# Expert slots of a two-layer diffusion backbone: the down products inside gate and up, two banks and two buffers for the rows, another order of the splits, and adaLN loads behind the reload of X

## The reference

```python
def _moe(h, router_w, router_bias, w_gate, w_up, w_down):
    ...
    for e in range(N_EXPERTS):
        he = jax.nn.silu(h @ w_gate[e]) * (h @ w_up[e])
        y = y + comb[:, e:e + 1] * (he @ w_down[e])
    return y
...
    x = x + g1 * yx                                   # the mixer
    hx = _rmsnorm(x, norm_ffn[i]) * (1 + sc2) + sh2   # adaLN, per layer
    x = x + g2 * y                                    # the experts
```

## Time and profile before

| | |
|---|---|
| three runs | 1175.56, 1180.86, 1182.62 us |
| profiled execution | 1180.38 us, of which 1178.6 are its span |
| TensorE busy | 1097.4 us (93%), granted clock 0.973 on average |
| VectorE busy | 821.6 us (70%) |
| ScalarE busy | 497.7 us (42%) |
| GpSimd busy | 201.3 us (17%) |
| expert slots, layer 0 | from about 222 to 483 us |
| expert slots, layer 1 | from about 925 us to the end |

### The profile page before, as it was taken

How to read it: one execution, slowest core, us unless ns; L and a number is a source line. 1 busy time by engine, 2 the same in 40 slices (tenths; PEclk the granted TensorE clock), 3 DMA queues, 4 the chain that set the end, 5 groups by cost and what they waited for, 6 DMA issues and landing times.

```text
span 1178.6 us, 16659 instructions
## 1 busy us (share of the span) xinstructions
PE 1097.4 (93%) x4819; PEld 806.0 (68%) x4820; DVE 821.6 (70%) x985; ACT 497.7 (42%) x681; POOL 201.3 (17%) x139
## 2 busy tenths in 40 slices
PE   4999899899999999579999999999999999999993
PEld 2554347577777777257888888878887677767772
DVE  5896985788888988355344344453565888888884
ACT  5210214376767676431111111141223466656662
POOL 2111111123333234100000000000000123223341
PEclk9999899899999999879999999999999999999997
DMA  9869549566979981603632233313235877988742
GB/s 361 330 242 384 212 178 415 198 232 184 338 235 345 343 224 24 237 16 127 251 124 93 82 111 125 125 54 124 85 131 202 343 222 267 372 295 282 209 92 34
DMA packets 82538, 243.03 MB, mean 206 GB/s; under 512 B 10592, under 2 KB 35384, under 8 KB 73276
## 3 DMA queue, kind: packets, MB, share of 16 engines
q1 hardware_dynamic: 62436, 188.88, 42.1%
q0 software_dynamic: 18496, 48.31, 16.3%
q10 hardware_dynamic: 1560, 5.26, 1.2%
HBM read 220.39 MB, written 40.89 MB: 222 GB/s over the span
## 4 chain that ended last, share of the span: by engine, by line
PE 65%; DVE 11%; DMA 10%; issue 8%; ACT 2%; ACTq 2%; DVEq 1%; POOL 0%; POOLq 0%
PE PS L1954 15%; PE PS L1835 7%; PE PS L2061 7%; PE PS L2065 7%; PE PS L2062 7%; DMA out_dram<-YO,TOKI 6%; PE PS L1967 3%; DVE ACC L1134 3%; PE PS L1973 3%; PE PS L1944 3%; PE PS L1686 2%; PE PS L1648 2%; PE PS L1848 2%; DMA WAE<-in_w_ada_dram 1%; PE PS L1863 1%
## 5 line engine op out<-in xcount | busy, mean ns | idle before, releaser
L1455 DVE TENSOR_TENSOR WL<-RAW,WH 128x1024 fp32r<-128x1024 f32 x204 | 240.1, 1220 | 26.0 <-ACT WH L922 24.9
L922 ACT ACTIVATE WH<-RAW 128x1024 fp32r x196 | 196.6, 1052 | 50.2 <-issue 36.7
L1954 PE MATMUL PS<-WH,XTH 128*128 128x512 f32 x384 | 154.0, 401 | 8.9 <-DVE XTL L1448 4.7
L2061 PE MATMUL PS<-HTH,WINH 128*128 128x512 f32 x384 | 150.8, 393 | 5.7 <-DVE HTL L1568 5.4
L1954 PE MATMUL PS<-WH,XTL 128*128 128x512 f32 x384 | 150.3, 391 | 0.0
L2062 PE MATMUL PS<-HTL,WINH 128*128 128x512 f32 x384 | 149.9, 390 | 0.0
L1954 PE MATMUL PS<-WL,XTH 128*128 128x512 f32 x384 | 149.8, 390 | 0.0
L2065 PE MATMUL PS<-HTH,WINL 128*128 128x512 f32 x384 | 118.7, 390 | 0.0
L1954 PEld LDWEIGHTS PS<-WH,XTH 128*128 128x128 f32 x384 | 72.1, 188 | 27.3 <-issue 13.4
L648 POOL DMA_INDIRECT XG<-h_dram,TOKI x54 | 68.1, 1261 | 113.8 <-DVE TOKI L1405 55.1
L2061 PEld LDWEIGHTS PS<-HTH,WINH 128*128 128x128 f32 x384 | 72.3, 188 | 22.3 <-DVE HTL L1568 4.8
(11 more groups left out here) (247 smaller groups left out, 1811.4 us busy)
## 6 DMA issues: line engine op xcount, KB each, us to landing
RAW<-in_moe_w_gate_dram SPq DMA_DIRECT2D x32, 1024.0 KB
RAW<-in_moe_w_up_dram SPq DMA_DIRECT2D x32, 1024.0 KB
WDR<-in_moe_w_down_dram SPq DMA_DIRECT2D x32, 1024.0 KB
WA<-in_w_ada_dram SPq DMA_DIRECT2D x28, 1024.0 KB, 8.3
WAE<-in_w_ada_dram SPq DMA_DIRECT2D x12, 1024.0 KB, 9.7
WINR<-in_conv_w_in_dram SPq DMA_DIRECT2D x24, 512.0 KB, 3.8
SLAB<-in_w_ada_dram SPq DMA_DIRECT2D x8, 1024.0 KB, 10.5
X<-x_dram SPq DMA_DIRECT2D x16, 512.0 KB, 5.9
```

The costliest lines, as they stand in the source:

```text
L922: nc.scalar.activation(piece_of(WH[par], i), raw_piece(at, i), ACT.Copy).then_inc(w_high, 1)
L1455: V.tensor_tensor(piece_of(WL[par], i), raw_piece(e, i), piece_of(WH[par], i).bitcast(f32), ALU.subtract).then_inc(w_low, 1)
L1954: ins = T.matmul(bank(2), x[:, ch, :], w[par][:, :, ch, :], start=ch == 0 and i == 0, stop=ch == NC - 1 and i == 2)
L2061: T.matmul(bank(b), WINH[par][:, ch, :], HTH[:, ch, cols], start=ch == 0, stop=False)
```

## The change

TensorE: the row transposes run one slot further ahead (s+2), gate and up of odd and even slots write different banks (2 and 6), and their four pieces are spread: piece 0, hidden transposes of s-1, piece 1, down products of s-1, pieces 2 and 3, row transposes of s+2. XTH and XTL get a second buffer. ScalarE and VectorE take the splits in another order, all four weight pieces of s+1 in slot s, WDH and WDL of s instead of s-1. Behind layer 0's slots SP issues the two adaLN loads after the reload of X, VectorE waits for the bias only before the first adaLN sum, GpSimd's clearing of ACC waits for WDL's semaphore as well, and TensorE's mixer columns wait for all HE (bank 6 is theirs).

The diff, cut to its core (the prologues and the unrolled last slots follow the same order, and skipped slots raise the semaphores to match):

```diff
+    XTL = [XTL0, r.put("XTL1", [P, NC, P], f32r)]
+    XTH = [r.put("XTH0", [P, NC, P], f32r), XTH1]
+    def gated_bank(par):
+        return bank(6 if par else 2)
 # SP
                 sp.wait_ge(w_low, PIECES * MAX_SLOTS)
-                load_ada_pair(2, 0)
                 sp.wait_ge(moe_done, 1)
                 sp.wait_ge(cols_mm, 2)
                 for m in range(NT):
                     sp.dma_start(X[:, m, :], x_dram[0][m * P:(m + 1) * P, :]).then_inc(x_back[m], 16)
+                load_ada_pair(2, 0)
 # GpSimd
                 pool.wait_ge(yd_mm, MAX_SLOTS)
+                pool.wait_ge(wd_low, MAX_SLOTS)
                 bias_row(1, 2 * D)
 # ScalarE
+            def het_high_of(s):
                 act.wait_ge(he_tr, s + (b + 1))
                 nc.scalar.activation(HETF[:], bank(3)[:, P:2 * P], ACT.Copy).then_inc(het_full, 1)
                 nc.scalar.activation(HETH[:], bank(3)[:, 0:P], ACT.Copy).then_inc(het_high, 1)
             def slot(s, par):
-                down_high(s - 1)
-                weights_high(s + 1, 1 - par, (2, 3))
-                gate(s)
-                xt_high(s + 1)
-                weights_high(s + 2, par, (0, 1))
+                weights_high(s + 1, 1 - par, (0,))
+                het_high_of(s - 1)
+                weights_high(s + 1, 1 - par, (1, 2, 3))
+                down_high(s)
+                gate(s, par)
+                xt_high(s + 2, par)
 # VectorE
             def body(s, par, free=True):
-                e0, e1, e2 = expert_of(s - 1), expert_of(s + 1), expert_of(s + 2)
+                e0, e1 = expert_of(s), expert_of(s + 1)
+                weights_low(s + 1, 1 - par, e1, (0,))
                 het_split(s - 1)
-                down_low(s - 1, e0)
-                weights_low(s + 1, 1 - par, e1, (2, 3))
+                weights_low(s + 1, 1 - par, e1, (1, 2))
+                y_evac(s - 1, 1 - par, free)
+                weights_low(s + 1, 1 - par, e1, (3,))
+                down_low(s, e0)
                 gated(s, par)
-                xt_low(s + 1)
-                weights_low(s + 2, par, e2, (0, 1))
-                y_evac(s - 1, 1 - par, free)
+                xt_low(s + 2, par)
-                dve.wait_ge(bias_in, 32)
 ...
                 taps(0, 0)
+                dve.wait_ge(bias_in, 32)
                 ada_pair(0, 2, 0, False)
 # TensorE
+            def transposes(s, par, nth, first=False):
                 pe.wait_ge(gathered[layer][par], nth * 16)
+                if not first:
+                    pe.wait_ge(xt_dve, s + b0)
+            def gate_up(s, par, pieces=range(PIECES), first=False):
+                if 0 in pieces:
+                    if not first:
+                        pe.wait_ge(he_ready, s + (b0 - 1))
+                    pe.wait_ge(xt_act, s + (b0 + 1))
+                    pe.wait_ge(xt_dve, s + (b0 + 1))
+                for piece in pieces:
+                    pe.wait_ge(w_low, s * PIECES + (b0 * PIECES + piece + 1))
 ...
             def slot(s, par, next_nth, more=True, last=False):
                 e = expert_of(s - 1)
+                if not last:
+                    gate_up(s, par, (0,))
                 pe.wait_ge(he_ready, s + b0)
                 hidden_transposes(s - 1, 1 - par)
                 if not last:
-                    gate_up(s, par)
-                if more:
-                    transposes(s + 1, 1 - par, next_nth)
+                    gate_up(s, par, (1,))
                 pe.wait_ge(yo_ready, s + (b0 - 1))
                 down(s - 1, e)
+                if not last:
+                    gate_up(s, par, (2, 3))
+                if more:
+                    transposes(s + 2, par, next_nth)
 ...
-            gate_up(0, 0)
             transposes(1, 1, 1)
+            gate_up(0, 0, first=True)
+            transposes(2, 0, 2)
 ...
+                pe.wait_ge(he_ready, MAX_SLOTS)
                 mixer_columns()
```

More of the change, by code:

```diff
@@ L235, in backbone @@
     WL = [r.put(f"WL{i}", [P, 2, NC, FF], f32r) for i in range(2)]
-    XTL = r.put("XTL", [P, NC, P], f32r)
+    XTL0 = r.put("XTL0", [P, NC, P], f32r)
     SG = r.put("SG", [P, FF])
@@ L909, in _, with xt_high @@
             b = layer * MAX_SLOTS
-            def xt_high(s):
+            def xt_high(s, par):
                 act.wait_ge(xt_tr, s + (b + 1))
-                nc.scalar.activation(XTH[:].rearrange("p c n -> p (c n)"), bank(0, 2),
+                nc.scalar.activation(XTH[par][:].rearrange("p c n -> p (c n)"), bank(0, 2),
                                      ACT.Copy).then_inc(xt_act, 1)
@@ L952, in _ @@
                 act.wait_ge(he_ready, b)
-            nc.scalar.activation(SG[:], bank(2)[:, 0:FF], ACT.Silu).then_inc(silu_g, 1)
-            xt_high(1)
-            weights_high(2, 0, (0, 1))
+            nc.scalar.activation(SG[:], gated_bank(0)[:, 0:FF], ACT.Silu).then_inc(silu_g, 1)
+            xt_high(2, 0)
+            down_high(0, first=True)
             with act.Fori(0, ALWAYS) as i:
@@ L1443, in gated, with xt_low @@
                 dve.wait_ge(silu_g, s + (b + 1))
-                V.tensor_tensor(HE[par][:], SG[:], bank(2)[:, FF:2 * FF], ALU.mult).then_inc(he_ready, 1)
-            def xt_low(s):
+                V.tensor_tensor(HE[par][:], SG[:], gated_bank(par)[:, FF:2 * FF], ALU.mult).then_inc(he_ready, 1)
+            def xt_low(s, par):
                 dve.wait_ge(xt_act, s + (b + 1))
-                V.tensor_tensor(XTL[:].rearrange("p c n -> p (c n)"), bank(0, 2),
-                                XTH[:].rearrange("p c n -> p (c n)").bitcast(f32),
+                V.tensor_tensor(XTL[par][:].rearrange("p c n -> p (c n)"), bank(0, 2),
+                                XTH[par][:].rearrange("p c n -> p (c n)").bitcast(f32),
                                 ALU.subtract).then_inc(xt_dve, 1)
@@ L1945, in transposes @@
                 ins.then_inc(xt_tr, 1)
-            def gate_up(s, par):
-                pe.wait_ge(xt_act, s + (b0 + 1))
-                pe.wait_ge(xt_dve, s + (b0 + 1))
-                for ch in range(NC):
-                    if ch % 2 == 0:
-                        pe.wait_ge(w_low, s * PIECES + (b0 * PIECES + ch // 2 + 1))
-                    for i, (x, w) in enumerate(((XTH, WH), (XTH, WL), (XTL, WH))):
-                        ins = T.matmul(bank(2), x[:, ch, :], w[par][:, :, ch, :],
-                                       start=ch == 0 and i == 0, stop=ch == NC - 1 and i == 2)
-                ins.then_inc(gu_mm, 1)
+            def gate_up(s, par, pieces=range(PIECES), first=False):
+                if 0 in pieces:
+                    if not first:
+                        pe.wait_ge(he_ready, s + (b0 - 1))
[3 more added lines that the diff above has]
+                    pe.wait_ge(w_low, s * PIECES + (b0 * PIECES + piece + 1))
+                    for ch in (2 * piece, 2 * piece + 1):
+                        for i, (x, w) in enumerate(((XTH, WH), (XTH, WL), (XTL, WH))):
+                            ins = T.matmul(gated_bank(par), x[par][:, ch, :], w[par][:, :, ch, :],
+                                           start=ch == 0 and i == 0, stop=ch == NC - 1 and i == 2)
+                if PIECES - 1 in pieces:
+                    ins.then_inc(gu_mm, 1)
             def hidden_transposes(s, par):
@@ L1993, in _ @@
                 pe.wait_ge(mixer_ready, 1)
[L1994 removed]
+            transposes(0, 0, 1, first=True)
             keep_running(2, 4)
[L1996 removed]
             transposes(1, 1, 1)
+            gate_up(0, 0, first=True)
+            transposes(2, 0, 2)
             keep_running(2, 4)
             e = expert_of(0)
+            gate_up(1, 1, (0,), first=True)
             pe.wait_ge(he_ready, 1 + b0)
             hidden_transposes(0, 0)
[L2003 to L2004 removed]
+            gate_up(1, 1, (1,), first=True)
             down(0, e)
[L2006 removed]
+            gate_up(1, 1, (2, 3), first=True)
+            transposes(3, 1, 2)
+            slot(2, 0, 3)
             with pe.Fori(1, ALWAYS) as i:
                 slot(2 * i + 1, 1, i + 2)
[L2009 removed]
+                slot(2 * i + 2, 0, i + 3)
             used = slots_used(pe)
@@ L2020, in _ @@
             with pe.If(used > 2 * n):
-                slot(MAX_SLOTS - 2, 1, n + 2)
+                slot(MAX_SLOTS - 2, 1, 0, more=False)
                 slot(MAX_SLOTS - 1, 0, 0, more=False)
```

94 lines of the change are left out of this document (46 added, 48 removed).

## The result

The changed kernel takes **1191.74 us** (median of four runs, 1190.13 to 1194.56), the kernel before 1180.27 with the run taken beside it (1175.56 to 1182.62): a ratio of 1.0109, 95% interval 1.0082 to 1.0135. Forecast were 1196.7, range 1160 to 1211. The profiled execution took 1190.13 us, of which 1188.3 are its span, so it is compared with the span of 1178.6 before: 9.7 more.

What follows compares the result with a forecast made beforehand. TensorE, 93% busy, was taken to bound the kernel before; after the change, a ring through ScalarE at 10.55 us a slot. 1180.4 + 13.9 (layer 0) + 5.9 (layer 1) - 3.5 (behind layer 0) = 1196.7 us, range 1160 to 1211.

Steps and rivals of the forecast that it cites:

- Part 1: TensorE's own order in a slot: 9.77 us if nothing else waits, with 3.93 from row transposes to down products.
- Part 2: ScalarE's new order, the deciding term: down products 4.31 us after the row transposes; round 10.15, with extras 10.55.
- the ring: Row transposes, XTH, first WH, HETF, down products, 12 more products, next row transposes: one round per slot, 10.15 us.
- The loop's start: ScalarE's loop starting over every second slot, between XTH and WH: 0.6 us taken, 0.3 per slot.
- rare long waits: ScalarE's occasional long waits ahead of WH, no longer covered: about 0.1 us per slot.
- Part 3: VectorE's slot: HE done 12.6 us after the row transposes, just when wanted; level with the ring, no cost by itself.
- Part 4: Rows, gathers, stores: XTL wait goes, no cost; slot 3's row transposes at 245.7 and 948.5.
- Part 5: Ends of the expert stages: last YO 8.7 us after the last row transposes; layer 0 +13.9, layer 1 +5.9.
- Part 6: Behind layer 0's slots: loads 1.3, bias wait 1.0, clock 1.2, together -3.5 us; TensorE's new wait covered by 1.5.
- TensorE as the bound (1160): Rival: HETF is not held up by WH and the loop start, slots of 9.77 us, 1160 us; chance 0.22.
- the ring at its floor (1180): Rival: the loop's start is hidden by the wait for row transposes, round about 10.15 us, 1180 us; chance 0.23.
- VectorE falling behind (1211): Rival: VectorE's register loads and long waits add to ScalarE's, round 10.9 us, 1211 us; chance 0.1.

Runs made afterwards that it cites:

- e3: Changed kernel with ScalarE's HETF and HETH copies ahead of the first WH and VectorE's HETL ahead of its WL: 1170.88 us, ratio 0.993.
- e7: e1 with VectorE's last WL (piece 3) moved ahead of YO: 1173.02 us, ratio 0.9948.
- e2: Changed kernel with two WH copies instead of one ahead of HETF on ScalarE: 1238.29 us, ratio 1.0495.
- e4: Changed kernel with ScalarE's loop over the first eight pairs of slots written out: 1187.41 us, ratio 1.0079.
- e1: Changed kernel with gate-and-up piece 2 moved ahead of the down products on TensorE: 1191.96 us, ratio 1.0109.
- e10: Changed kernel with layer 1's down weights of experts 3 to 15 loaded for 16 columns of 1024, for measuring alone: 1193.69 us, ratio 1.0131.
- e11: Kernel before with layer 1's down weights of experts 3 to 15 loaded for 16 columns of 1024, for measuring alone: 1170.91 us, ratio 0.9935.
- e5: Kernel before with only the two adaLN loads moved behind the reload of X and the bias wait moved to the first adaLN sum: 1175.35 us, ratio 0.9966.
- e6: Changed kernel with the adaLN loads and the bias wait left as in the kernel before: 1196.97 us, ratio 1.0143.
- e8: e3 with GpSimd's gather of slot s+5 ahead of the store of slot s: 1171.24 us, ratio 0.9931.
- e12: e3 with VectorE's last WL (piece 3) ahead of YO: 1167.72 us, ratio 0.9921.
- e9: e3 with layer 1's down weights of experts 3 to 15 loaded for 16 columns of 1024, for measuring alone: 1165.64 us, ratio 0.9899.

## Why the prediction was right

The mechanism named as deciding was the one that decided. The range by itself says little, as it was wide enough for every rival; what confirms the forecast is the signs it gave: TensorE idle for HETF in front of the down products (0.23 and 0.63 us in turn, where I had written 0.4 and 1.0), slots of 10.5 us, and no wait for XTL. The sum by its steps:

- **Part 1**, TensorE's own 9.77 us: 9.78 in e3 and e7, in the plain loops, where nothing else binds.
- **Part 2**, the ring. T to XTH 1.09 forecast, 1.07 measured; to WH 1.70, measured 1.72; to HETF 1.00, measured 0.96; to the down products 0.52, measured 0.53: 4.31 against 4.28. The down products then took 3.20 and not 3.10 (their first row 1.98 where it was 1.88), the last 12 products 2.75: 10.23, forecast 10.15. The loop's start was the term mis-sized: 0.40 where I took 0.6, between the bounds of 0.22 and 0.9. The two errors offset each other: 10.42 in the plain loops, forecast 10.45. e2 (longer ring, slower), e3 (ring opened, 9.78) and e4 (loop's start removed) show it from three sides.
- The last 0.1 of the round, rare long waits, held by luck. The stages' means of 10.50 and 10.49 are 0.08 above 10.42, but from another cause: no idle time of ScalarE ahead of the first WH in the plain loops was over 1.16 us. The 0.08 is mostly the loops with an If, whose start cost 0.7 to 0.9 and not 0.40 (idle 1.36 to 1.63 there against 0.69).
- The sentence on the Trainium skill, "Runtime: NRT & Kernel Launch", section "Instruction fetch mechanics": a stall of 1.2 us at every loop start (a size from my longest wait, the page gives none), which would have made 1205, was not there. The extra is 0.40 in the plain loops and up to 0.9 in those with an If; whether fetching instructions is in it, no run shows.
- **Part 3**, VectorE "level with the ring": too pessimistic by 0.9. HE starts at T + 11.23 in the changed kernel (302.81 to 314.04) and so ends near T + 11.65, not 12.6. Up to HETL the forecast held (T + 5.1, forecast 5.2). The step that failed is the next, "ScalarE reaches that WH 1.21 after HETH (register loads)": a misreading of the earlier trace rows. The row of 276.54 is WDH, so the 1.21 is WDH's copy (1.06) and 0.15 of idle time. The change moves WDH behind the four WH, and only 0.23 us lies between HETH and the second WH. YO is at T + 7.77, not 8.7. At the end of each layer it was at T + 8.6 after all (471.01 to 479.61, 1163.28 to 1171.88), as ScalarE there paused 0.78 and 0.94 us between HETH and the next WH; so Part 5's 8.7 held by luck. e1 is the price of the same gap in my picture: I knew one ring, and a step later the second, through YO, binds at nearly the same length.
- **Part 4**: right for the changed kernel, by e10. T of slot 3 came 23.18 us after the first transposes, forecast 23.56. That transfers are no limit is true only of slots this long; I hadn't seen that 0.2 of the 10.06 us of layer 1 before was traffic (e11).
- **Part 5**, measured from the first transposes: layer 0's YO +12.5 (forecast 13.9), layer 1's +4.8 (5.9).
- **Part 6**: -2.9 in the trace, -3.6 to -5 by e5 and e6, forecast -3.5; right in size, not in its terms.
  - *The loads* gave more than the 1.3 forecast, in two ways. From the reload's first command to the first square took 3.4 us where it took 5.3. And the last store landed sooner, a term I had at nothing: from YO to the clearing of ACC 8.98 us against 10.62. The second is most likely the loads' doing too. In the two traces that issue them beside the last store (before, and e11) that stretch is 10.62 and 10.66, in e5, with the slots of before and the loads moved, 8.37, and in the other traces with the new slots' order 8.65 to 8.98. e6, with the loads still ahead of the reload, is no exception with 8.65: it issued them only 0.6 us before the stores were in. (e8 is left out, as its last store comes behind a gather.)
  - *TensorE's new wait* took some 0.4 of it back. The mixer's columns began 8.1 us behind YO (forecast 9) but ended at 488.85, behind the stores' landing (9.0 after YO, forecast 10.6); the reload waited for them and started at 488.95, 0.36 behind the clearing, where before it started with it. SP's wait names the columns' line (51.6 us are from SP's command before):

```profile
SPq L582 <- PE PS L1689: 51.6, 1, 51.6
```

  - *The bias wait* no longer holds VectorE: the step behind the first four squares followed them at once, where WINL held it up by 1.0 before. But the four squares themselves took 6.4 us and not 5.2, waiting for the tiles of X, so nothing was left of it. Why the tiles came more slowly, no run shows.
  - *The clock* gave nothing: 0.54 granted over the first 8 us of the convolution's transposes against 0.50.

The rivals: TensorE as the bound (1160) and the ring at its floor (1180) are refuted by the 21.2 us in front of the down products and the 0.40 at every loop start. VectorE falling behind (1211) is not so in the changed kernel, but was near: e1 is that case. The rule of the Trainium skill that speaks for that first rival ("Perfetto Trace Analysis", "Optimizing Tensor Performance") is met by e3 and e12, which beat the kernel before with the same two banks; whether the banks or the second buffer for rows bring it, no run here separates.

## What to carry to other kernels

When a consumer is moved nearer to its producer, add up the whole chain round the loop, engine by engine and with each queue's preamble, and compare it with the busiest engine's own time: here waits of 0.23 and 0.63 us a slot, for a copy of 0.28 us queued behind one of 1 us, left the kernel 11 us slower than before, and taking the short copy first won 21. Before reading a distance between two rows as a wait, look at which instruction lies in it: my 1.21 us of register loads were another copy. Opening one ring shows the next one, so list the waits that stand ahead of long work in each in-order queue before choosing the move. A faster stage meets limits that the slower one hid, here the memory traffic of layer 1.

## What the runs showed of the hardware

- Stores and gathers land late together with the weights' loads. After 100 us at 303 GB/s with the DMA engines 88% busy, e3's TensorE waited 2.65 us for rows and its YO 2.12 for a store; in e9, at 240 GB/s and 75%, TensorE waited for rows only at the start of layer 1 (up to 2.0 us) and YO never.
- One adding store beside two loads of 1 MB landed later: from the last store of layer 0 to the clearing of ACC, which waits for it, 8.44 us in the kernel before and 8.48 in e11, which issue the loads 1.4 us behind the store, against 6.20 in e5, which has them behind the reload.
- The granted clock of the convolution's first 8 us does not follow the idle time just before it. The changed kernel's TensorE idled 2.24 us there and had been granted 1.00 from 501 to 508, and was granted 0.54; e3 idled 2.56 and was granted 0.79; the kernel before idled 10.60 and was granted 0.50; e11 idled 11.67 and was granted 0.71.
- Writing ScalarE's loop out saves more than the loop's start: the pause ahead of WH went from 0.69 to 0.52 in the slots that had no loop start, too.
